# Expert products split by the parity of the input step, 512 columns wide, in a two-layer encoder trunk on one core

## The chip, the cores and the metric

The kernel runs on one core of one Trainium2 chip. The metric is the device time of one execution in microseconds (us); lower is better. Everything is computed in float32.

## What is computed

Two layers over 256 tokens of 1024 features: attention of three kinds with a projection in and out, then a mixture of 32 experts, of which each token uses two. The attention part matters here only as the work ahead of the experts; the experts are these lines of the reference:

```python
    g_p, g_sel = lax.top_k(g_prob, 1)
    ...
    e_p, e_sel = lax.top_k(jax.nn.softmax(e_logits, axis=-1), TOP_K_IN_GROUP)
    gate = g_p * e_p / jnp.sum(e_p, axis=-1, keepdims=True)
    ...
    def expert_block(args):
        xb, e = args
        h = jax.nn.silu(xb @ w_gate[e]) * (xb @ w_up[e])
        return h @ w_down[e]
    ...
    out = jax.ops.segment_sum(y, stok, num_segments=n)
```

`w_gate` and `w_up` are 1024 x 512 per expert, `w_down` is 512 x 1024. After the second layer the result is normalised and written out.

## The kernel before

Each layer has an attention stage and an expert stage. In the expert stage the 32 experts are taken in 4 rounds of 8 (`ROUNDS`, `BODY`), each round in two quads of 4 experts. Every expert has room for 32 tokens (`CAP`), so that the four experts of a quad fill 128 rows. There is a loop for experts with more than 32 tokens, which is entered only if there is one.

The order of the work is written out by hand, engine by engine, with semaphores between them. For an expert, TensorE (PE) does this, and in this order with the neighbours (lines 1909 to 1915): `products(e)`, `down_of(e - 1)`, `turned(e)`, `add(e - 1)`.

- `gate_up` (L1754 to L1771): for each of the 8 steps j of the input, four products with the same 32 tokens, each in its own group of 32 columns of the array and on its own 32 partitions of the bank `gu_ps`. The groups i = 0, 1 make the two halves of the gate's outputs, i = 2, 3 those of up, 256 columns each. So every group sums over all 8 steps.
- ScalarE (ACT) copies `gu_ps` to `h_rows`; `turns` (L1773) turns it by two transposes (L1777), and by two more products (L1779) the gate weights of this expert; ACT takes the exponential (L819), VectorE (DVE) makes silu times up in `hidden` (L1230 to L1233), then copies the turned gate weights to four groups of 32 partitions (L1236).
- `down` (L1783): for each of 4 chunks of the hidden vector, four groups of 32 columns, each with 256 of the 1024 outputs, into `tr`. ACT copies the result to `y` (128 x 256).
- `scatter` (L1794, products at L1799): for each of two tiles of 128 tokens, four products over 32 rows each, one for each 256 outputs, added to the sums that live in the four banks of `pj` and `lg` during the whole stage. A bank holds 256 outputs of both token tiles.

The sums are opened by `zero_sum` (L1701, products at L1703, which mark each bank as written) and `open_sum` on ACT (L774), which copies x in. The queue of SyncE (SP) issues the loads of the weights. An expert is 6144 KB. There are three places in the ring and one late place; experts 0 to 3 are loaded during attention. Expert 4's input half follows piece by piece as the first expert's steps are used (`REFILLS`, L503 to L507), and from then on a load waits for `gu_used` and `d_used` of the expert that held its place: ACT signals `d_used` when `down` of that expert has ended (L848). Two pieces of `w_down` of expert 2 lie where x lay and wait for `sums_open` and `rows_ready` (L498 to L501).

The last expert's `w_down` comes in four pieces of 512 KB with semaphores of their own (`last_in`, L577, L1787). After the last `scatter`, ACT and DVE read the sums: between the layers they copy them back to x (L889, L1330), which PE turns for the next layer (`turn_in`, L1464, L1470) once all is there, and at the end they square and weigh them in turns, half by half (L894, L1337). At two places per layer PE runs products of zeros, `keep_warm` (L1730).

Of the kernel before, what the change touches and what calls it, by code (L numbers as in the profile page):

```python
# [20 lines left out]
ALU = mybir.AluOpType  # L21
# [192 lines left out]
def trunk(nc, x_d, w_in_d, w_out_d, norm_mix, norm_ffn, bias_d, lam_q1, lam_k1, lam_q2, lam_k2,  # L214
# [3 lines left out]
    with ctx:  # L218
# [16 lines left out]
        h_ps = pv[:, 1, 0:2 * P].rearrange("p (c h s) -> p c h s", c=HALF // P, h=4)  # L235
# [31 lines left out]
        zeros = sb("zeros", P + 512, BF16)  # L267
# [51 lines left out]
        h_rows = take(HALF)  # L319
        y = take(D_MODEL // QUAD)  # L320
# [7 lines left out]
        hid = take(2 * P).rearrange("p (b c h s) -> p b c h s", b=2, c=HALF // P, h=2)  # L328
        e_neg = take(P).rearrange("p (c n) -> p c n", c=HALF // P)
        over_k = take(OVER)  # L330
        one0, cnt = over_k[:, 0:N_EXPERTS], over_k[:, N_EXPERTS:2 * N_EXPERTS]
        flags = lam_in.rearrange("p v d -> p (v d)")[:, 0:N_EXPERTS * MORE]
        codes = take(OVER)
        assert taken[0] <= 2048
        taken[0] = 2048
# [3 lines left out]
        chosen = take(TOK * N_EXPERTS).rearrange("p (t e) -> p t e", t=TOK)  # L339
        low = ARENA - 2 * SLOT - D_MODEL  # L340
# [20 lines left out]
        last_in = [sem(f"last_in{k}") for k in range(KE)]  # L361
# [102 lines left out]
        def _(sp):  # L464
# [3 lines left out]
            def first_experts(l):  # L468
# [46 lines left out]
            for l in range(DEPTH):  # L515
# [27 lines left out]
                for m in range(ROUNDS):  # L543
# [19 lines left out]
                    for kind, e in loads_of(m):  # L563
# [82 lines left out]
        def _(act):  # L646
# [20 lines left out]
            for l in range(DEPTH):  # L667
# [106 lines left out]
                def open_sum(t, half):  # L774

                    act.wait_ge(sums_zeroed, at(l, 4, 2 + 2 * half))
                    act.wait_ge(x_added, at(l, PARTS, (2, PARTS)[t] if half == 0 else 2 + t))
                    return copy(acc[t][half], x[:, t, 512 * half:512 * half + 512].rearrange("p (i c) -> p i c", i=2))
# [14 lines left out]
                for t in range(TOK):  # L793
# [4 lines left out]
                    else:  # L798
# [4 lines left out]
                        open_sum(0, 0)  # L803
# [14 lines left out]
                def neg_exp(b):  # L818
                    return nc.scalar.activation(e_neg, h_ps[:, :, 0:2, :].rearrange("p c h s -> p c (h s)"),  # L819
# [1196 lines left out]
```

## Time and profile before

| | us |
|---|---|
| median of 3 runs | 1163.73 |
| lowest and highest | 1161.87, 1165.86 |
| the profiled execution | 1163.3 |
| its span | 1161.4 |

| engine | busy us | share of the span |
|---|---|---|
| TensorE products (PE) | 923.6 | 80% |
| TensorE weight loads (PEld) | 581.4 | 50% |
| VectorE (DVE) | 417.7 | 36% |
| ScalarE (ACT) | 212.4 | 18% |

The profile was taken from one execution, which took 1163.3 us, 1.9 us more than its span. In the trace a float32 product appears as two matrix instructions, each with a weight load. A row of the timeline has the start and the length in us, the engine and the line, then the operation, what it writes and reads, its shape (rows x columns of the array, then partitions x columns of the moving operand) and the count; in brackets stands how long the engine was idle before it and what ended that.

### The profile page before, as it was taken

The numbers are of one execution on the slowest core, as the hardware profiler recorded it, in microseconds if no ns is written. First come the engines' busy times: TensorE is split into PE (matmuls) and PEld (weight loads), VectorE is DVE, ScalarE is ACT, GpSimd is POOL, SyncE is SP. The second block draws the span as 40 slices with busy tenths as digits, with TensorE's granted clock in tenths as the row PEclk, the third lists the DMA queues.
The fourth block names the chain that finished last, engine by engine and source line by source line (L and its number), as shares of the span: only waits on it lengthen the run. The fifth ranks groups of instructions, "written<-read, shape, count | busy, mean of one in ns | idle before, by whom it ended". The sixth has DMA issues, their size and how long they took to land.

```text
span 1161.4 us, 22055 instructions
## 1 busy us (share of the span) xinstructions
PE 923.6 (80%) x9540; PEld 581.4 (50%) x9547; DVE 417.7 (36%) x1180; ACT 212.4 (18%) x623; POOL 16.3 (1%) x38
## 2 busy tenths in 40 slices
PE   9999999776766576668899999997585857566786
PEld 5876666453434343435468766654343524334443
DVE  3656554421231222222337464554222222222223
ACT  2234332010101010101112442310110101001012
POOL 1000000000000000000010000000000000000000
PEclk9999999987888889879999999999888978898799
DMA  7966499999999999999996466999999999999996
GB/s 305 414 239 246 192 392 437 421 430 433 431 431 433 431 429 428 432 424 417 424 393 239 163 240 250 402 432 432 430 431 431 429 433 433 428 430 425 421 421 276
DMA packets 28116, 445.04 MB, mean 383 GB/s; under 512 B 8944, under 2 KB 10352, under 8 KB 14832
## 3 DMA queue, kind: packets, MB, share of 16 engines
q1 hardware_dynamic: 27456, 443.49, 90.6%
q8 instruction: 78, 1.28, 0.4%
q10 hardware_dynamic: 560, 0.10, 0.0%
q14 instruction: 22, 0.18, 0.0%
HBM read 442.53 MB, written 1.05 MB: 382 GB/s over the span
## 4 chain that ended last, share of the span: by engine, by line
DMA 50%; PE 45%; issue 1%; DVE 1%; ACT 1%; SPq 1%; POOL 0%; POOLq 0%; ACTq 0%; DVEq 0%
DMA ring_xb<-in_experts 44%; PE pv L1766 12%; PE pj L1391 8%; PE tr L1789 5%; DMA arena<-in_experts 3%; DMA ring_xb<-in_w_in_chunks 3%; PE pj L1397 2%; PE pj L1501 2%; PE pj L1621 2%; PE pj L1596 1%; PE pj L1799 1%; PE pj L1630 1%; PE lg L1421 1%; PE tr L1431 1%; PE pv L1779 1%
## 5 line engine op out<-in xcount | busy, mean ns | idle before, releaser
L1766 PE MATMUL pv<-ring_xb,xT 128*32 128x256 f32 x3840 | 286.8, 459 | 174.1 <-DMA ring_xb<-in_experts 173.9
L1766 PEld LDWEIGHTS pv<-ring_xb,xT 128*32 128x32 f32 x3840 | 136.2, 127 | 312.3 <-DMA ring_xb<-in_experts 189.9
L1230 DVE TENSOR_SCALAR arena<-arena 128x128 f32<-128x128 f32 x64 | 14.6, 228 | 562.7 <-ACT arena L819 562.7
L1789 PE MATMUL tr<-ring_xb,arena 128*32 128x256 f32 x1920 | 115.4, 379 | 17.8 <-issue 15.1
L649 ACT ACTIVATE arena<-pv 128x256 f32<-128x256 f32 x64 | 24.6, 385 | 491.2 <-PE pv L1766 491.2
L1236 DVE COPY arena<-pv 32x256 f32<-32x256 f32 x256 | 105.5, 412 | 2.6
L1391 PE MATMUL pj<-xT,ring_xb 128*128 128x256 f32 x448 | 100.1, 381 | 0.0
L1789 PEld LDWEIGHTS tr<-ring_xb,arena 128*32 128x32 f32 x1920 | 63.9, 109 | 61.2 <-issue 19.6
L1391 PEld LDWEIGHTS pj<-xT,ring_xb 128*128 128x128 f32 x448 | 84.1, 190 | 13.1 <-issue 1.1
L1799 PE MATMUL pj<-arena 32*128 32x256 f32 x512 | 72.5, 399 | 6.7 <-ACT arena L649 5.4
L1748 PE MATMUL tr<-arena,rows 128*128 128x128 f32 x448 | 60.6, 300 | 15.2 <-issue 10.5
L1799 PE MATMUL lg<-arena 32*128 32x256 f32 x512 | 72.5, 400 | 0.0
L649 ACT ACTIVATE arena<-tr 128x256 f32<-128x256 f32 (+3 forms) x106 | 41.3, 407 | 151.1 <-PE tr L1789 128.9
L1748 PEld LDWEIGHTS tr<-arena,rows 128*128 128x128 f32 x448 | 58.0, 213 | 20.1 <-issue 14.7
L1231 DVE RECIPROCAL arena<-arena 128x128 f32<-128x128 f32 x64 | 61.0, 953 | 2.2
L1799 PEld LDWEIGHTS pj<-arena 32*128 32x128 f32 x512 | 44.5, 184 | 23.2 <-issue 19.7
L649 ACT ACTIVATE xT<-tr,gains 128x128 f32<-128x128 f32 x128 | 36.6, 369 | 75.7 <-PE tr L1748 73.5
L1799 PEld LDWEIGHTS lg<-arena 32*128 32x128 f32 x512 | 43.7, 184 | 0.0
L1779 PE MATMUL pv<-con,arena 128*32 128x128 f32 x256 | 40.0, 279 | 0.0
L1777 PE MATMUL pv<-con,arena 128*128 128x128 f32 x128 | 32.4, 335 | 9.5 <-ACT arena L649 9.5
L1777 PEld LDWEIGHTS pv<-con,arena 128*128 128x128 f32 x128 | 20.3, 207 | 37.3 <-issue 19.8
L649 ACT ACTIVATE arena<-pj 64x256 f32<-64x256 f32 (+2 forms) x48 | 21.0, 442 | 72.7 <-PE pj L1391 52.2
(228 smaller groups left out, 807.5 us busy)
## 6 DMA issues: line engine op xcount, KB each, us to landing
ring_xb<-in_experts SPq DMA_DIRECT2D x48, 6144.0 KB, 22.1
ring_xb<-in_experts SPq DMA_DIRECT2D x18, 2048.0 KB, 13.3
ring_xb<-in_experts SPq DMA_DIRECT2D x6, 4096.0 KB, 28.0
ring_xb<-in_w_in_chunks SPq DMA_DIRECT2D x10, 2048.0 KB, 19.5
ring_xb<-in_w_out_halves SPq DMA_DIRECT2D x4, 2048.0 KB, 29.9
arena<-in_experts SPq DMA_DIRECT2D x2, 4096.0 KB, 12.8
ring_xb<-in_experts SPq DMA_DIRECT2D x8, 1024.0 KB, 9.6
arena<-in_experts SPq DMA_DIRECT2D x4, 2048.0 KB, 37.9
```

The source lines that it names most:

```text
L649: return nc.scalar.activation(out, in_, ACT.Copy, **k)
L1231: own.link(v.reciprocal(e_neg, e_neg))
L1236: ins = v.tensor_copy(pgT[k * CAP:(k + 1) * CAP, b].rearrange("p t s -> p (t s)"), pgt_ps[0:CAP])
L1391: ins = mm(out, w[:, j], xT[:, j, :], start=(j == 0), stop=(j == KD - 1))
L1397: ins = mm(out, src[:, j, t * P:(t + 1) * P], weights(i, n)[:, j, c:c + m], start=(j == 0), stop=(j == KD - 1))
L1501: ins = mm(bank[:, 0:R5], xT_raw[:, j, t * P:(t + 1) * P], weights(0, n5)[:, j, :], start=(j == 0), stop=(j == KD - 1))
L1748: ins = mm(wide_ps[:, j * n:(j + 1) * n], rows[:, t, j * P:(j + 1) * P], pick[:, t, 0:n], start=(t == 0), stop=(t == TOK - 1))
L1766: ins = mm(gu_ps[i * CAP:(i + 1) * CAP, :], xg[:, j, c:c + CAP], w, start=(j == 0), stop=(j == KD - 1), tile_position=(0, i * CAP), skip_g ...
L1777: turn_(h_ps[:, c].rearrange("p h s -> p (h s)"), by_step[:, c], ident)
L1779: ins = mm(pgt_ps[0:CAP, t * P:(t + 1) * P], pgate[:, t, i, :], ident, start=True, stop=True, tile_position=(0, 0), skip_group_check=True)
L1789: ins = mm(tr[i * CAP:(i + 1) * CAP, 0, 0:SEQ], hid[:, b, k % 2, k // 2, :], rows_of[k][:, SEQ * i:SEQ * (i + 1)], start=(k == 0), stop=(k ...
L1799: ins = mm(sums[i][:, SEQ * t:SEQ * (t + 1)], pgT[r, b, t, :], y[r, :], start=False, stop=last, tile_position=(i * CAP, 0), skip_group_che ...
```

## The change

- `gate_up`: each step makes two products of 512 columns, gate and up, in the column groups 0 and 2 on even steps and 1 and 3 on odd ones. Each group now sums over half the steps.
- `turns`: instead of two transposes, four products with `join`, a 128 x 64 matrix that turns a chunk of 128 and adds the two partial sums. The gate weights of a quad are turned once, at its first expert, for all four. `h_rows` and `y` are 512 wide.
- `down`: each chunk makes two products of 512 columns, again in groups by parity, and `scatter` multiplies over 64 rows, so that the two partial sums are added in it: one product per token tile and half.
- The sums: a bank holds one token tile and one half of the outputs. Three of the four `zero_sum` products go, since the banks are marked by earlier products, whose start flags are changed for that; a smaller one stays. `open_sum` for the upper halves is moved ahead of the second token tile's work on ACT, and `sums_open` is signalled once, after the lower halves.
- The last expert: the last piece of `w_down` is split in two, the lower half of the outputs is copied out and scattered ahead of the upper one, and what reads the sums waits for the bank it reads. At the end ACT and DVE take the banks in another order.
- `e_neg` goes (`hid` is used), `zeros` shrinks from 128 x 640 to 128 x 128 and is read repeatedly, and three products of zeros at the program's start go (L1487 to L1489).

```diff
-        sums = (pj[:, 0], pj[:, 1], lg[:, 0], lg[:, 1])
-        acc = tuple(tuple(bank[:, :, SEQ * t:SEQ * (t + 1)] for bank in (pj, lg)) for t in range(TOK))
+        acc = tuple(tuple(bank[:, t] for bank in (pj, lg)) for t in range(TOK))
-        gu_ps = pv[:, 0, 0:HALF]
+        gu_ps = pv[:, 0]
...
-        zeros = sb("zeros", P + 512, BF16)
+        zeros = sb("zeros", P, BF16)
...
-                    sp.wait_ge(sums_open, at(l, TOK, t + 1))
+                    sp.wait_ge(sums_open, l + 1)
...
-                            for k in range(KE):
+                            for k in range(KE - 1):
                                 sp.dma_start(spare[k], down_v[n][:, k]).then_inc(last_in[k], 16)
+                            for side in range(2):
+                                there = slice(512 * side, 512 * side + 512)
+                                sp.dma_start(spare[KE - 1][:, there], down_v[n][:, KE - 1, there]).then_inc(last_in[KE - 1 + side], 16)
...
                         open_sum(1, 0)
-                        open_sum(0, 0)
+                        open_sum(0, 0).then_inc(sums_open, 1)
...
-                    if t == 1:
-                        open_sum(0, 1).then_inc(sums_open, 1)
-                        open_sum(1, 1).then_inc(sums_open, 1)
-                    else:
+                    if t == 0:
+                        open_sum(0, 1)
+                        open_sum(1, 1)
                         gate_exps(0)
...
+                    def last_y_out(e):
+
+                        act.wait_ge(lower_down, l + 1)
+                        copy(y[0:64], tr[0:64, 0]).then_inc(lower_y, 1)
+                        act.wait_ge(wide_done, at(r, WIDE, y_use(e)))
+                        act.sem_inc(d_used[place(m * BODY + e)], 1)
+                        copy(y[64:128], tr[64:128, 1]).then_inc(wide_read, 1)
...
-            for t, half, weighted_first in ((0, 1, 0), (0, 0, 1), (1, 0, 1), (1, 1, 3)):
+            act.wait_ge(acc_done, at(DEPTH - 1, 2 * TOK, 1))
+            for t, half, weighted_first in ((0, 0, 0), (0, 1, 1), (1, 1, 1), (1, 0, 3)):
...
-                    for t, half, squared_first in ((0, 0, 0), (0, 1, 1), (1, 1, 1), (1, 0, 3)):
+                    dve.wait_ge(acc_done, at(l, 2 * TOK, TOK + 1))
+                    for t, half, squared_first in ((0, 1, 0), (0, 0, 1), (1, 0, 1), (1, 1, 3)):
...
-                if l == 0:
-                    for _ in range(3):
-                        mm(lg[:, 0], zeros[:, 0:P], zeros[:, P:P + 512], start=True, stop=True)
...
-                        for i in range(4):
-                            w = both[:, j, D_EXPERT * (i // 2):D_EXPERT * (i // 2 + 1)].rearrange("p (d c) -> p d c", c=KE)[:, :, KE // 2 * (i % 2):KE // 2 * (i % 2) + KE // 2]
-                            ins = mm(gu_ps[i * CAP:(i + 1) * CAP, :], xg[:, j, c:c + CAP], w,
-                                     start=(j == 0), stop=(j == KD - 1), tile_position=(0, i * CAP),
-                                     skip_group_check=True)
+                        for g in range(2):
+                            i = 2 * g + j % 2
+                            ins = mm(gu_ps[i * CAP:(i + 1) * CAP, :], xg[:, j, c:c + CAP],
+                                     both[:, j, D_EXPERT * g:D_EXPERT * (g + 1)], start=(j < 2), stop=(j >= KD - 2),
+                                     tile_position=(0, i * CAP), skip_group_check=True)
...
+                def turns(quad):
+
+                    by_chunk = h_rows.rearrange("q (p k) -> q k p", k=KE)
+                    for k in range(KE):
+                        ins = mm(h_ps[:, k].rearrange("p g s -> p (g s)"), by_chunk[:, k], join, start=True, stop=True,
+                                 skip_group_check=True)
+                    if quad:
+                        for t in range(TOK):
+                            ins = mm(pgt_ps[:, t * P:(t + 1) * P], pgate[:, t].rearrange("p e s -> p (e s)"), ident,
+                                     start=True, stop=True, skip_group_check=True)
+                    return ins
+
+                def down_part(rows_of, b, k, side, bank):
+
+                    i = 2 * side + k % 2
+                    return mm(tr[i * CAP:(i + 1) * CAP, bank], hid[:, b, k, :], rows_of[k][:, 512 * side:512 * side + 512],
+                              start=(k < 2), stop=(k >= KE - 2), tile_position=(0, i * CAP), skip_group_check=True)
...
+                def scatter_part(b, t, side, last):
+
+                    r = slice(64 * side, 64 * side + 64)
+                    return mm(acc[t][side], pgT[r, b, t, :], y[r, :], start=False, stop=last, tile_position=(64 * side, 0),
+                              skip_group_check=True)
```

Where the order moves: PE in the first expert stage, from `products(2)` on, with `down_of(1)`, `turned(2)` and `add(1)`. Before:

```order
L1766 MATMUL pv<-ring_xb,xT 32x256 [waits gu_full2]
L1766 MATMUL pv<-ring_xb,xT 32x256 x31
L1789 MATMUL tr<-ring_xb,arena 32x256 [waits wide_read,hid_ready,d_full1]
L1789 MATMUL tr<-ring_xb,arena 32x256 x15
L1777 MATMUL pv<-con,arena 128x128 [waits pgt_read,gu_read]
L1777 MATMUL pv<-con,arena 128x128
L1779 MATMUL pv<-con,arena 32x128 x2
L1799 MATMUL pj<-arena 128x256 [waits wide_read,pgt_read]
L1799 MATMUL pj<-arena 128x256
L1799 MATMUL lg<-arena 128x256 x2
L1799 MATMUL pj<-arena 128x256 x2
L1799 MATMUL lg<-arena 128x256 x2
```

The same place with the change (in it `gate_up` is L1785, `down` L1807, `turns` L1796 and `scatter` L1831):

```order
L1785 MATMUL pv<-ring_xb,xT 32x512 [waits gu_full2]
L1785 MATMUL pv<-ring_xb,xT 32x512 x15
L1807 MATMUL tr<-ring_xb,arena 32x512 [waits wide_read,hid_ready,d_full1]
L1807 MATMUL tr<-ring_xb,arena 32x512 x7
L1796 MATMUL pv<-arena 128x64 [waits pgt_read,gu_read]
L1796 MATMUL pv<-arena 128x64 x3
L1831 MATMUL pj<-arena 128x512 [waits wide_read,pgt_read]
L1831 MATMUL lg<-arena 128x512
L1831 MATMUL pj<-arena 128x512
L1831 MATMUL lg<-arena 128x512
```

The 60 products of an expert become 32, and the order of the four parts stays.

ACT ahead of the first expert, from the second tile's rows back to the first tile's (the copies `lg<-ring_xb` and `pj<-ring_xb` are `open_sum`). Before:

```order
L649 ACTIVATE rows<-ring_xb,rms 128x64x8
L788 ACTIVATE arena,lam_product<-arena,lam_product 128x4 [waits gmax_ready]
L791 ACTIVATE lam_product<-best 128x1 [waits emax_ready]
L649 ACTIVATE arena<-pj 128x512 [waits xnT_done]
L649 ACTIVATE xT<-tr 128x2x128 [waits xnT_done] x2
L649 ACTIVATE pj<-ring_xb 128x2x256 [waits x_added,sums_zeroed] x2
L649 ACTIVATE rows<-ring_xb,rms 128x64x8 [waits rms_ready,x_added]
L649 ACTIVATE rows<-ring_xb,rms 128x64x8
L649 ACTIVATE lg<-ring_xb 128x2x256 [waits x_added,sums_zeroed] x2
L649 ACTIVATE xT<-tr,gains 128x128 [waits wide_done]
```

With the change:

```order
L652 ACTIVATE rows<-ring_xb,rms 128x64x8
L652 ACTIVATE lg<-ring_xb 128x512 [waits x_added,mix_read,lg_read] x2
L796 ACTIVATE arena,lam_product<-arena,lam_product 128x4 [waits gmax_ready]
L799 ACTIVATE lam_product<-best 128x1 [waits emax_ready]
L652 ACTIVATE arena<-pj 128x512 [waits xnT_done]
L652 ACTIVATE xT<-tr 128x2x128 [waits xnT_done] x2
L652 ACTIVATE pj<-ring_xb 128x512 [waits x_added,xnT_read,sums_zeroed] x2
L652 ACTIVATE rows<-ring_xb,rms 128x64x8 [waits rms_ready,x_added]
L652 ACTIVATE rows<-ring_xb,rms 128x64x8
L652 ACTIVATE xT<-tr,gains 128x128 [waits wide_done]
```

The two copies to `lg` have moved ahead of the gate's exponentials, and nothing stands any more between the last `rows` copy and the first gathered tokens.

PE at the last expert of a layer, from its `down` on, with the change (before, the four pieces had four products of 256 columns each, and the eight products of `scatter` followed, all behind one wait for `y`):

```order
L1807 MATMUL tr<-xT,arena 32x512 [waits last_in0,wide_read,hid_ready]
L1807 MATMUL tr<-xT,arena 32x512
L1807 MATMUL tr<-arena 32x512 [waits last_in1]
L1807 MATMUL tr<-arena 32x512
L1807 MATMUL tr<-lowrank,arena 32x512 [waits last_in2]
L1807 MATMUL tr<-lowrank,arena 32x512
L1807 MATMUL tr<-arena 32x512 [waits last_in3]
L1807 MATMUL tr<-arena 32x512 [waits last_in4]
L1831 MATMUL pj<-arena 128x512 [waits lower_y,pgt_read]
L1831 MATMUL pj<-arena 128x512
L1831 MATMUL lg<-arena 128x512 [waits wide_read]
L1831 MATMUL lg<-arena 128x512
```

The last two rows of `scatter` wait for the upper half alone.

## Rows read from the trace of the kernel before

**Rows 1.** The profile's page: GB/s by slice, the queue that loads instructions

```profile
GB/s 305 414 239 246 192 392 437 421 430 433 431 431 433 431 429 428 432 424 417 424 393 239 163 240 250 402 432 432 430 431 431 429 433 433 428 430 425 421 421 276
...
q8 instruction: 78, 1.28, 0.4%
```

**Rows 2.** The chain of waits in order of time: start, length, what

```profile
202.78 19.51 DMA ring_xb<-in_experts
...
543.63 38.29 DMA ring_xb<-in_w_in_chunks
```

**Rows 3.** Windows: stretch, its us, busy of PE, PEld, DVE, ACT, POOL, clock, DMA share, GB/s

```profile
155.00:160.00 5.00, 4.90 (x63) 3.36 (x66) 2.70 (x15) 3.69 (x13) 0.00 (x0) 1.00 0.81 238
730.00:735.00 5.00, 4.90 (x63) 3.33 (x66) 2.79 (x16) 3.52 (x13) 0.00 (x0) 1.00 0.94 338
230.00:520.00 290.00, 194.94 (x2426) 116.11 (x2430) 73.20 (x187) 31.32 (x97) 0.00 (x0) 0.83 1.00 429
```

**Rows 4.** Timeline, PE on experts 3 to 5, and a gather in the last round

```profile
193.17 0.61 PE L1789 MATMUL tr<-xT,arena 128*32 128x256 f32 x8
...
195.00 0.51 PE L1777 MATMUL pv<-con,arena 128*128 128x128 f32 x2
...
195.99 0.48 PE L1799 MATMUL pj<-arena 32*128 32x256 f32 x2
...
197.07 3.83 PE L1766 MATMUL pv<-ring_xb,xT 128*32 128x256 f32 x64
...
200.72 1.91 PE L1789 MATMUL tr<-ring_xb,arena 128*32 128x256 f32 x32
...
1101.00 3.84 PE L1748 MATMUL tr<-arena,rows 128*128 128x128 f32 x32
```

**Rows 5.** Timeline at the second expert: tiles of two kinds of products side by side

```profile
162.77 0.43 PE L1766 MATMUL pv<-ring_xb,xT 128*32 128x256 f32 x3
...
162.87 0.27 PE L1779 MATMUL pv<-con,arena 128*32 128x128 f32 x1
```

**Rows 6.** Timeline, the load of expert 7 and PE at expert 6, both layers

```profile
207.82 1.51 PE L1766 MATMUL pv<-ring_xb,xT 128*32 128x256 f32 x16 [3.13 <-DMA ring_xb<-in_experts]
777.60 0.33 SPq L570 DMA_DIRECT2D ring_xb<-in_experts  x1
781.98 1.51 PE L1766 MATMUL pv<-ring_xb,xT 128*32 128x256 f32 x12 [2.47 <-DMA ring_xb<-in_experts]
```

**Rows 7.** Loads and stores by line: times, KB each, median us from issue to landing

```profile
out<-rows SPq DMA_DIRECT2D x2, 512.0 KB, 3.1
```

**Rows 8.** Timeline, SP's loads ahead of the first experts

```profile
155.54 2.37 SPq L501 DMA_DIRECT2D ring_xb<-in_experts  x2
...
157.96 2.12 SPq L505 DMA_DIRECT2D ring_xb<-in_experts  x3
```

**Rows 9.** Timeline, the program's start

```profile
5.50 1.49 PE L1489 MATMUL lg<-zeros 128*128 128x512 bf16 x3
...
15.73 0.61 PE L1484 MATMUL lg<-arena,con 128*128 128x128 f32 x4
```

**Rows 10.** Timeline, ACT copying 512 columns out of `tr`

```profile
136.23 0.60 ACT L649 ACTIVATE arena<-tr 128x512 f32<-128x512 f32 x1
```

**Rows 11.** Timeline, from the last expert of layer 0 to layer 1

```profile
574.82 0.64 PE L1789 MATMUL tr<-xT,arena 128*32 128x256 f32 x8
...
581.96 6.17 PE L1501 MATMUL pj<-ring_xb,rows 128*128 128x440 f32 x16 [0.39 <-DMA ring_xb<-in_w_in_chunks]
```

**Rows 12.** Timeline, the end of layer 1

```profile
1149.14 0.64 PE L1789 MATMUL tr<-xT,arena 128*32 128x256 f32 x8
...
1150.49 0.64 PE L1789 MATMUL tr<-arena 128*32 128x256 f32 x8
1151.28 0.39 ACT L649 ACTIVATE arena<-tr 128x256 f32<-128x256 f32 x1 [3.37 <-PE tr L1789]
...
1155.12 0.60 ACT L894 ACTIVATE arena<-lg 128x512 f32<-128x512 f32 x1
```

More of the change, by code:

```diff
@@ L1212, in weigh @@
                     own.mark(v.tensor_copy(cnt, pv[:, 1, 64:96]))
+                    groups = ident.rearrange("p (g j s) -> p g j s", g=2, j=2)
+                    own.mark(v.tensor_tensor(join.rearrange("p (g s) -> p g s", g=2), groups[:, :, 0, :], groups[:, :, 1, :], ALU.add))
                     rank(1)
@@ L1462, in _ @@
                 for _ in range(8 if l == 0 else 4):
[L1463 removed]
+                    mm(tr[:, 0].rearrange("p (n c) -> p n c", n=KE), zeros, spread(zeros, 1, KE), start=True, stop=True)
                 def turn_in(t):
@@ L1699, in gather_first @@
                     return ins
-                def zero_sum(i):
-                    mm(sums[i], zeros[:, 0:P], zeros[:, P:P + 512], start=True, stop=False,
-                       skip_group_check=True).then_inc(sums_zeroed, 1)
                 out_upper(1, 1)
@@ L1732, in keep_warm @@
                     for _ in range(n):
-                        mm(sums[0], zeros[:, 0:P], zeros[:, P:P + 512], start=False, stop=False,
+                        mm(pj[:, 0].rearrange("p (n c) -> p n c", n=KE), zeros, spread(zeros, 1, KE), start=False, stop=False,
                            skip_group_check=True)
@@ L1771, in gate_up @@
                     return ins
-                def turns(i):
-                    by_step = h_rows.rearrange("q (p c) -> q c p", c=HALF // P)
-                    for c in range(HALF // P):
-                        turn_(h_ps[:, c].rearrange("p h s -> p (h s)"), by_step[:, c], ident)
-                    for t in range(TOK):
-                        ins = mm(pgt_ps[0:CAP, t * P:(t + 1) * P], pgate[:, t, i, :], ident, start=True, stop=True,
-                                 tile_position=(0, 0), skip_group_check=True)
-                    return ins
@@ L1794, in scatter @@
-                def scatter(b, last=False):
-                    for t in range(TOK):
-                        for i in range(4):
-                            r = slice(i * CAP, (i + 1) * CAP)
-                            ins = mm(sums[i][:, SEQ * t:SEQ * (t + 1)], pgT[r, b, t, :], y[r, :],
-                                     start=False, stop=last, tile_position=(i * CAP, 0), skip_group_check=True)
-                            if last and t == TOK - 1:
-                                ins.then_inc(acc_done, 1)
+                def turns(quad):
[8 more added lines that the diff above has]
+                    return ins
@@ new lines, in down @@
+                def down(rows_of, b):
+                    for k in range(KE):
+                        for side in range(2):
+                            ins = down_part(rows_of, b, k, side, 0)
+                    return ins
+                def scatter_part(b, t, side, last):
+                    r = slice(64 * side, 64 * side + 64)
+                    return mm(acc[t][side], pgT[r, b, t, :], y[r, :], start=False, stop=last, tile_position=(64 * side, 0),
+                              skip_group_check=True)
@@ L1803, in scatter @@
+                def scatter(b):
+                    for t in range(TOK):
+                        for side in range(2):
+                            ins = scatter_part(b, t, side, False)
                     return ins
@@ L1875, in add, with down_and_add_last @@
                         if m == 0 and e == 0:
-                            pe.wait_ge(sums_open, at(l, TOK, TOK))
-                        scatter(e % 2, m == ROUNDS - 1 and e == BODY - 1)
+                            pe.wait_ge(sums_open, l + 1)
+                        scatter(e % 2)
+                    def down_and_add_last(e):
+                        pe.wait_ge(hid_ready, at(r, BODY, e + 1))
+                        pe.wait_ge(wide_read, at(r, READS, y_read(e) - 1))
+                        down_last(e % 2)
+                        pe.wait_ge(pgt_read, at(r, BODY, e + 1))
+                        pe.wait_ge(lower_y, l + 1)
+                        for side in range(2):
+                            if side == 1:
+                                pe.wait_ge(wide_read, at(r, READS, y_read(e)))
+                            for t in range(TOK):
+                                scatter_part(e % 2, t, side, True).then_inc(acc_done, 1)
                     if m == ROUNDS - 1:
```

130 lines of the change are left out of this document (71 added, 59 removed).

## The prediction

> **What bounds the kernel now.** I read the page first. Its GB/s by slice are near 430 in most slices and fall to 163 to 250 in two stretches, the attention stages [rows 1]; from 230 to 520 us the transfers run at 429 GB/s with their engines busy all the time, while PE is busy 195 of 290 us [rows 3]. The chain of waits says the same from the end: in the expert stages its long pieces are loads of `experts`, and one of 38.3 us (the weights of the next layer) leads into layer 1 [rows 2]. So an expert costs what its 6144 KB take, 6.29 MB / 429 GB/s = 14.7 us, and what PE saves in that stretch is waiting time. PE sets the time in five places only: the program's start and the attention stages; the first steps of the first expert, which free the ring; the first six experts, four of them already loaded, which PE takes at its own pace while each frees the place of a later one; the way from the last expert into layer 1; and the end.
>
> **The change, part by part,** against the profiled execution (1163.3 us, span 1161.4; the median of the runs is 0.4 above it).
>
> *PE per expert.* Matrix instructions in four column groups run four at a time: in `down` 32 of 256 columns take 1.91 and 8 take 0.61, so 24 more take 1.30, or 0.43 for eight, and 0.18 is the tail [rows 4]. `gate_up` has 64 in 3.83 [rows 4]. With the change it has 32 of twice the length, and four neighbours still lie in four groups (0, 2, 1, 3): 32 x 0.108 + 0.18 = 3.65, which saves 0.18. `down` keeps its array time, 1.9. The four parts of `turns` took 195.99 - 195.00 = 0.99; eight instructions with full weights at the gather's 3.84 / 32 = 0.12 make 0.96, and at the first expert of a quad four more, 0.48 [rows 4]. `scatter` took 197.07 - 195.99 = 1.08 [rows 4] with 16 instructions in four row groups, 0.86 of it array time at the rate above. Over 64 rows only two groups exist: two rows of four instructions, 0.43 each, make 1.72. That is 0.86 more. Sum: -0.18 - 0.03 + 0.86 = +0.65 us per expert, so PE becomes slower, not faster. In the loading stretch, with some 4 us or more idle per expert, this costs nothing.
>
> That two 64-row products overlap at all is seen on no row; the nearest are the column groups above. The Trainium skill (TensorEngine Tiling (Array Packing), Tiling Modes) gives two tiles for 64 rows and four for 32, so by it too this product loses half of its overlap.
>
> *The burst of the first six experts.* The load of expert 7 waits for `down` of expert 4. Until then PE has done six `gate_up` (-1.1), five `turns` (-0.15 and twice +0.48) and four `scatter` (+3.4): +3.1. The load was issued at 202.78 in layer 0 [rows 2] and at 777.60 in layer 1, and the load ahead of it had landed when PE began expert 6, at 207.82 and 781.98 [rows 6]. The 512 KB output takes 3.1 us to land, of which 1.2 is transfer, so a load needs some 1.9 ahead [rows 7]. It must be issued by 205.9 and 780.1; with +3.1 it comes at 205.9 and 780.7. I take +0.5 for both layers; bounds 0 and, with PE 1.5 slower per expert in place of 0.65, +4 per layer.
>
> *Earlier loads ahead of the burst.* SP issued the two pieces over x at 155.54, behind the sums' opening, and the first refills at 157.96 [rows 8]. From 155 to 160 only 238 GB/s flowed, which is 5 x (429 - 238) / 429 = 2.2 us lost, and 1.1 in 730 to 735 [rows 3]. With the lower sums opened first, the pieces can go after 152.5 and 154.6. But the refills behind them still wait for the first steps of `gate_up`, whose 512-column products end some 0.4 later. The gap moves more than it closes: -0.3 per layer, bounds 0 and the whole 3.3. The products of zeros and the copies that go or move here lie beside the router's chain on DVE and PE.
>
> *The start.* Three products of zeros (1.49) go, but at 15.73 PE needs a product of x's norm, which DVE and ACT make from a load of x and not from PE's work [rows 9]. I take it that this norm comes some 0.3 ahead of PE: -0.3, bounds 0 and -1.5.
>
> *Into layer 1.* `y` of 512 columns takes ACT 0.60 in place of 0.39 [rows 10, 12]. So `scatter` of the last but one expert starts 0.2 later and takes 0.86 longer: `down` of the last starts at 574.82 + 1.1 = 575.9 [rows 11]. Its four chunks go in two pairs of 0.86: results at 577.8. ACT copies both halves by 579.1, `scatter` of the upper half ends about 580.3 and 581.1, the copies back at 581.0 and 581.8, and PE turns the second tile (8 x 0.12 and a tail) from about 582.0: layer 1 starts at 583.1, not at 581.96 when its weights landed [rows 11]. +1.1; bounds -0.4 (the idle time there) and +2.
>
> *The end.* Before, `down` of the last expert started at 1149.14, its last piece came at 1150.49, and the last sum was squared from 1155.12 [rows 12]. Now, as in layer 0, `down` from 1150.15, results at 1152.0, two copies to 1153.4, the lower `scatter` from 1152.9 and the upper beside it from 1153.5 to 1155.4. The first square starts at 1154.0, but three more in turns with DVE follow the upper half, the last from 1156.8: +1.7. The last piece's arrival no longer decides, so splitting it buys nothing. Bounds: -0.5 (half a piece) and +3.
>
> The upper `scatter` can start beside the lower only if tiles overtake. They do: three instructions of `gate_up` start at 162.77, ahead of an L1779 at 162.87 that precedes them in the program [rows 5]. The Trainium skill (TensorE: Matmul & The Clock Gate, The mechanism) says that matmuls start and end strictly in program order. By that the upper one would wait for the lower one's last start, and this term would be +2.3; the row differs, and I go by it.
>
> *Instructions loaded.* They are 1.28 MB in all [rows 1]; about a fifth go: -0.3 us, bounds 0 and -1.
>
> **Sum:** +0.5 - 0.6 - 0.3 + 1.1 + 1.7 - 0.3 = **+2.1**, that is 1165.4 for the profiled execution and **1165.8** for the median. A measurement of this kernel tells about 0.3%, 3.5 us, from no change.
>
> **The rivals.**
>
> *Faster: the ring is what counts.* If the early pieces close the gaps (-3.3), PE is not late for expert 7 (0), the start gives -1.3, and both ends are set by arrivals as now (+0.3 together), the sum with the instructions' -0.3 is about -4.6: 1159.1. For it: the 238 GB/s, and the idle 0.39 for DMA ahead of layer 1 [rows 11]. Against it: the refills behind the pieces, and 1.1 us more work on PE ahead of the last `down`. 0.18.
>
> *Slower: expert 7's load.* Between `down`, `turns`, `scatter` and `gate_up` the array changes its division four times per expert. If that, or a slower 64-row product, makes an expert 1.5 us longer than before, `down` of expert 4 is over 7 us later, and transfers stand still for about 4.5 in each layer: 1165.8 + 8 = 1174. It decides from about 3 us of lateness on, and the forecast is at 3.1. Before, the changes cost little: 0.2 between `scatter` and `gate_up`. The Trainium skill (TensorEngine Tiling (Array Packing), Key Properties) says that a change of tiling mode drains the engine; it gives no price. 0.18.
>
> *Slower: the groups do not overlap at 512 columns.* Then `gate_up` takes about 6.9 and `down` 3.4, an expert costs 12.7 of PE's time, the burst is some 26 us longer, less 3 of slack: 23 per layer, near 1213. Nothing speaks for it except that neighbours now have different weights. 0.04.
>
> **How the numbers follow.** The forecast has 0.60; rivals 0.18, 0.18, 0.04. Of the forecast, 0.02 lies under -3.5 and 0.06 over +3.5: faster 0.20, same 0.52, slower 0.28. The range takes in most of the first two rivals and the bounds of the terms near the ends: 1159.5 to 1172.
>
> **What would show it.** Right: `gate_up` at 3.6 to 3.7 warm, `down` 1.9, `scatter` 1.7 to 1.9; PE's busy time little changed though its instructions fall by nearly half; the GB/s in the long stretch still 429; the load of expert 7 three us later after the first `gate_up` than before; PE, not a load, ahead of layer 1; and 12 to 13 us between the landing of the last piece and the end (now 11). Wrong: a gap in GB/s behind expert 6, or PE waiting for the last piece again.

## The result, and the profile after

The changed kernel takes **1181.9 us** (median of 4 runs, 1181.67 to 1183.22) against 1163.18 beside it: a ratio of 1.0157, 95% interval 1.0144 to 1.0170, or 18.7 us. The forecast was 1165.8 with a range up to 1172. Further down, the numbers in brackets behind a time are its ratio to the kernel before, measured beside it, and the 95% interval of that ratio.

| | before | after |
|---|---|---|
| span of the profiled execution | 1161.4 | 1180.0 |
| PE busy | 923.6 | 1031.4 |
| instructions, all engines | 22055 | 15268 |
| ACT busy | 212.4 | 240.9 |

PE executes far fewer instructions and is busy 108 us longer. The page of the changed kernel, with its GB/s to be held against [rows 1]:

```profile
PE 1031.4 (87%) x6146; PEld 552.2 (47%) x6146; DVE 423.9 (36%) x1182; ACT 240.9 (20%) x625; POOL 15.8 (1%) x38
...
GB/s 307 402 234 264 206 390 404 347 436 436 428 432 433 436 429 425 436 425 424 421 393 199 167 204 289 398 336 421 424 435 429 435 429 434 434 431 428 430 423 218
```

The eighth slice fell from 421 to 347 (and the seventh from 437 to 404), and one of layer 1 from 432 to 336. The windows of the changed kernel, with the columns of [rows 3], show the two places, the long stretch, and the pieces ahead of the burst:

```profile
200.00:204.00 4.00, 4.00 (x26) 2.82 (x20) 0.00 (x0) 1.09 (x3) 0.00 (x0) 1.00 0.97 418
204.00:208.00 4.00, 4.00 (x32) 1.19 (x32) 3.71 (x9) 0.08 (x1) 0.00 (x0) 1.00 0.19 78
208.00:212.00 4.00, 4.00 (x33) 1.75 (x25) 2.10 (x8) 1.19 (x2) 0.00 (x0) 1.00 0.00 0
...
200.00:220.00 20.00, 20.00 (x144) 8.75 (x136) 10.95 (x30) 3.23 (x7) 0.00 (x0) 1.00 0.65 264
780.00:800.00 20.00, 20.00 (x148) 8.94 (x144) 8.68 (x23) 3.66 (x9) 0.00 (x0) 1.00 0.64 255
...
230.00:520.00 290.00, 232.60 (x1436) 107.64 (x1424) 75.94 (x189) 40.28 (x99) 0.00 (x0) 0.88 1.00 431
...
155.00:160.00 5.00, 4.90 (x40) 2.78 (x44) 2.93 (x17) 2.65 (x11) 0.00 (x0) 1.00 0.88 322
```

Read the last column. Before, both 20 us stretches ran at 427 GB/s:

```profile
200.00:220.00 20.00, 15.56 (x220) 8.91 (x212) 10.86 (x31) 2.10 (x6) 0.00 (x0) 0.91 1.01 427
780.00:800.00 20.00, 14.57 (x214) 8.29 (x214) 8.94 (x27) 1.43 (x4) 0.00 (x0) 0.91 1.00 427
```

So 20 x (427 - 264) / 427 = 7.6 us of transfer are lost in layer 0 and 8.1 in layer 1, at expert 7's load. PE is busy throughout both. The long stretch stands at 431 GB/s as before, though PE works 233 of its 290 us and not 195 [rows 3]. The timeline says why the burst is late. One expert of it, to be held against [rows 4], and the issue of expert 7's load in each layer:

```profile
164.49 3.64 PE L1785 MATMUL pv<-ring_xb,xT 128*32 128x512 f32 x32
167.95 1.90 PE L1807 MATMUL tr<-ring_xb,arena 128*32 128x512 f32 x16
169.78 2.08 PE L1796 MATMUL pv<-arena 128*128 128x64 f32 x8
171.79 0.69 PE L1831 MATMUL pj<-arena 64*128 64x512 f32 x1
...
173.18 0.59 PE L1831 MATMUL pj<-arena 64*128 64x512 f32 x1
...
211.12 0.33 SPq L570 DMA_DIRECT2D ring_xb<-in_experts  x1
...
794.71 0.33 SPq L570 DMA_DIRECT2D ring_xb<-in_experts  x1
```

L1785 is `gate_up`, L1807 `down`, L1796 the join in `turns`, L1831 `scatter`. The join holds PE for 171.79 - 169.78 = 2.01 us, where the forecast had 0.96. `scatter` takes 1.91, `gate_up` 3.46 from start to start. The next expert begins at 173.70, 9.21 us behind 164.49; over the whole burst it is 9.21 to 9.22. Before, an expert took 7.56, from this row to 197.07 [rows 4]:

```profile
189.51 3.83 PE L1766 MATMUL pv<-ring_xb,xT 128*32 128x256 f32 x64
```

By expert 4's `down` that makes the load 8.3 us late (211.12, not 202.78 [rows 2]).

The rest is at the end. In windows of 2 us the expert transfers die out between 1148 and 1152 before (the first two rows) and between 1162 and 1166 after (the other two), 14 us later; the span grew by 18.6:

```profile
1148.00:1150.00 2.00, 1.94 (x32) 1.32 (x36) 0.02 (x1) 0.00 (x0) 0.00 (x0) 1.00 0.56 221
1150.00:1152.00 2.00, 1.32 (x24) 0.51 (x20) 0.00 (x0) 0.39 (x1) 0.00 (x0) 1.00 0.14 57
...
1162.00:1164.00 2.00, 2.00 (x18) 0.42 (x16) 1.87 (x5) 0.00 (x0) 0.00 (x0) 1.00 0.64 246
1164.00:1166.00 2.00, 1.11 (x8) 0.55 (x6) 1.43 (x4) 0.60 (x1) 0.00 (x0) 1.00 0.22 88
```

So about 4.6 lie behind the last transfer:

```profile
1145.36 1.92 PE L1807 MATMUL tr<-ring_xb,arena 128*32 128x512 f32 x16 [0.64 <-DMA ring_xb<-in_experts]
1147.22 2.08 PE L1796 MATMUL pv<-arena 128*128 128x64 f32 x8
...
1151.15 2.33 PE L1753 MATMUL pj<-zeros 128*128 128x512 bf16 x10
1153.41 1.92 PE L1785 MATMUL pv<-arena,xT 128*32 128x512 f32 x16
1155.27 1.47 PE L1753 MATMUL pj<-zeros 128*128 128x512 bf16 x6
1156.66 1.92 PE L1785 MATMUL pv<-arena,xT 128*32 128x512 f32 x16
1159.39 2.08 PE L1796 MATMUL pv<-arena 128*128 128x64 f32 x8 [0.80 <-ACT arena L652]
```

From 1145.36 on no row of PE waits for a transfer. The products of `keep_warm` (L1753), which filled waits before, now stand in PE's way, and the join is there twice. `keep_warm` has three places at the end of a layer, not two: ten, six and four products.

### The profile page after: what moved, and what is told of

Same layout as the page of the kernel before. It is cut to its first block, busy times and chain, and to the rows that moved or that the text cites. A ratio compares the mean times of both kernels' runs of the same rounds, so it can differ in the third digit from the quotient of the medians.

```text
span 1180.0 us, 15268 instructions
## 1 busy us (share of the span) xinstructions
PE 1031.4 (87%) x6146; PEld 552.2 (47%) x6146; DVE 423.9 (36%) x1182; ACT 240.9 (20%) x625; POOL 15.8 (1%) x38
## 4 chain that ended last, share of the span: by engine, by line
PE 56%; DMA 40%; issue 1%; ACT 1%; DVE 1%; SPq 0%; POOL 0%; POOLq 0%; ACTq 0%; DVEq 0%
DMA ring_xb<-in_experts 39%; PE pv L1785 14%; PE pj L1420 8%; PE tr L1807 7%; PE pv L1796 4%; PE pj L1831 4%; PE pj L1426 2%; PE tr L1767 2%; PE pj L1647 2%; PE pj L1527 1%; PE pj L1622 1%; PE pj L1656 1%; PE lg L1450 1%; DMA ring_xb<-in_x 1%; ACT arena L652 1%
## 5 line engine op out<-in xcount | busy, mean ns | idle before, releaser
L1785 PE MATMUL pv<-ring_xb,xT 128*32 128x512 f32 x1920 | 269.8, 711 | 102.9 <-DMA ring_xb<-in_experts 102.7
L1785 PEld LDWEIGHTS pv<-ring_xb,xT 128*32 128x32 f32 x1920 | 65.1, 127 | 283.4 <-issue 147.3
L1796 PEld LDWEIGHTS pv<-arena 128*128 128x128 f32 x512 | 124.3, 327 | 67.6 <-ACT arena L652 65.9
L1796 PE MATMUL pv<-arena 128*128 128x64 f32 x512 | 133.2, 403 | 12.8 <-ACT arena L652 12.8
L1831 PE MATMUL pj<-arena 64*128 64x512 f32 x256 | 130.8, 632 | 9.0 <-ACT arena L652 9.0
L1831 PE MATMUL lg<-arena 64*128 64x512 f32 x256 | 131.1, 633 | 0.0
L1807 PE MATMUL tr<-ring_xb,arena 128*32 128x512 f32 x960 | 114.5, 595 | 5.7 <-issue 3.8
L652 ACT ACTIVATE arena<-tr 128x512 f32<-128x512 f32 (+4 forms) x108 | 56.1, 537 | 144.1 <-PE tr L1807 121.8
L1831 PEld LDWEIGHTS pj<-arena 64*128 64x128 f32 x256 | 44.1, 191 | 52.8 <-issue 48.4
L1807 PEld LDWEIGHTS tr<-ring_xb,arena 128*32 128x32 f32 x960 | 29.6, 110 | 83.6 <-issue 79.8
L1831 PEld LDWEIGHTS lg<-arena 64*128 64x128 f32 x256 | 44.1, 191 | 0.5 <-issue 0.5
```

The costliest lines, as they stand in the source:

```text
L652: return nc.scalar.activation(out, in_, ACT.Copy, **k)
L1785: ins = mm(gu_ps[i * CAP:(i + 1) * CAP, :], xg[:, j, c:c + CAP], both[:, j, D_EXPERT * g:D_EXPERT * (g + 1)], start=(j < 2), stop=(j >= KD ...
L1796: ins = mm(h_ps[:, k].rearrange("p g s -> p (g s)"), by_chunk[:, k], join, start=True, stop=True, skip_group_check=True)
L1807: return mm(tr[i * CAP:(i + 1) * CAP, bank], hid[:, b, k, :], rows_of[k][:, 512 * side:512 * side + 512], start=(k < 2), stop=(k >= KE - 2 ...
L1831: return mm(acc[t][side], pgT[r, b, t, :], y[r, :], start=False, stop=last, tile_position=(64 * side, 0), skip_group_check=True)
```

## The experiments

**Theory A:** the join is dear because its weights lie 16 bytes apart; this and `scatter` slow the burst, expert 7's load comes late, and transfers stand still. **Rivals:** B, the join is dear because its products are short or full-sized between narrow tiles; C, PE's longer work costs by itself, and the gap is only its shadow.

### The join's weights

The first edit lets ACT lay `h_rows` down chunk by chunk:

```diff
-                        copy(h_rows, gu_ps).then_inc(gu_read, 1)
+                        copy(h_rows.rearrange("q (k p) -> q p k", k=KE), gu_ps.rearrange("q (p k) -> q p k", k=KE)).then_inc(gu_read, 1)
...
-                    by_chunk = h_rows.rearrange("q (p k) -> q k p", k=KE)
+                    by_chunk = h_rows.rearrange("q (k p) -> q k p", k=KE)
```

> The changed kernel, but ACT writes h_rows chunk by chunk, so that the join's weights lie side by side instead of 16 bytes apart. Theory A (the stride of the weights makes the join dear, 0.26 us an instruction, and the long burst releases expert 7's load late): the eight join instructions fall from 2.08 us to 0.95 to 1.05, an expert of the burst from 9.22 to 8.15, expert 7's load is issued at 205.8 instead of 211.1, about 2.4 us of transfer are lost in each layer instead of 7.7 to 8.0, and with 1 us at each layer's way out the time is 1167 to 1170. Rival B (the join is dear because its products are short or because full and narrow tiles alternate, not because of the stride): join still 2.0 us or more, time 1181 to 1183.

Measured: 1169.78 us (1.0056, 1.0040 to 1.0073). The join takes 1.03 to the next start, an expert 8.24, the load is issued at 206.63. **12.1 us of the 18.7 come back by one access pattern.** Rival B is out. PE's weight loads for the join show it by themselves, in the changed kernel and in this run: 327 ns each against 191.

```profile
L1796 PEld LDWEIGHTS pv<-arena 128*128 128x128 f32 x512 | 124.3, 327 | 67.6 <-ACT arena L652 65.9
...
L1796 PEld LDWEIGHTS pv<-arena 128*128 128x128 f32 x512 | 61.9, 191 | 75.0 <-ACT arena L652 73.3
```

Lost transfers were more than expected: both stretches ran at 352 GB/s, 3.5 us each.

The same by itself, on the array alone, behind the last `scatter`:

```diff
                         down_and_add_last(BODY - 1)
+                        if l == DEPTH - 1:
+                            by4 = h_rows.rearrange("q (p k) -> q k p", k=4)
+                            by2 = h_rows.rearrange("q (p k) -> q k p", k=2)
+                            by1 = h_rows.rearrange("q (k p) -> q k p", k=4)
+                            for _ in range(4):
+                                mm(pv[:, 0, 0:64], by1[:, 0], join, start=True, stop=True)
...
```

> The changed kernel with nine groups of four products behind its last scatter, on the same h_rows, whose result nobody reads: weights side by side, 8 bytes apart, 16 bytes apart, each with 64 columns of join, with 128 columns of ident, and as transposes. Theory A: an instruction with weights side by side takes 0.11 to 0.14 us whatever the columns, with 16 bytes apart 0.25 to 0.26, with 8 bytes apart between the two or like 16. Rival B: 64 columns cost no less than 0.25 with weights side by side too. Time about 10 us over the changed kernel's.

The probe's timeline; the lines stand in the order by1, by2, by4, for 64 columns, for 128, and as transposes:

```profile
1171.39 1.10 PE L1987 MATMUL pv<-arena 128*128 128x64 f32 x8
1172.34 1.11 PE L1989 MATMUL pv<-arena 128*128 128x64 f32 x8
1173.28 2.03 PE L1991 MATMUL pv<-arena 128*128 128x64 f32 x8
1175.14 1.11 PE L1993 MATMUL pv<-con,arena 128*128 128x128 f32 x8
1176.09 1.11 PE L1995 MATMUL pv<-con,arena 128*128 128x128 f32 x8
1177.03 2.03 PE L1997 MATMUL pv<-con,arena 128*128 128x128 f32 x8
1178.90 0.60 PE L1999 MATMUL pv<-con,arena 128*128 128x128 f32 x4
1179.33 0.64 PE L2001 MATMUL pv<-con,arena 128*128 128x128 f32 x4
1179.81 0.64 PE L2003 MATMUL pv<-con,arena 128*128 128x128 f32 x4
```

From start to start, eight instructions take 0.95 us with weights side by side, 0.94 with weights 8 bytes apart and 1.86 with 16 bytes: 0.12, 0.12 and 0.23 us each, the same for 64 and 128 columns. That 8 bytes cost nothing was not expected. Four transposes take 0.43 and 0.48 to the next start with the turned data side by side and 8 bytes apart, and the row for 16 bytes is as long as the one for 8 (0.64). So the old `turns` (L1777 in [rows 4]), transposes that read 8 bytes apart, could not have shown it. The probe's 1182.52 us, 0.6 over the changed kernel and not 10, is no price: its products lie beside the kernel's tail on other engines.

The Trainium skill (Advanced Engine Details and Errata, Memory Cachelines) says that SBUF is read in lines of 16 bytes and that at least two accesses must fall into a line to hide its latency. The trace agrees for weights: two float32 in a line are free, one in a line costs twice.

In that first mending ACT wrote with a jump of 512 bytes between elements, and its copy took 1.08 us. The other walk, `q k p` on both sides, reads PSUM 16 bytes apart and writes in a row:

> As join_contiguous, but ACT walks h_rows in the order it is written and PSUM 16 bytes apart; in join_contiguous it wrote 16-byte neighbours 512 bytes apart and took 1.08 us where the copy took 0.60. In best_try the copy of this form took 0.60. Theory A: join 0.95 and copy 0.60, an expert of the burst as in join_contiguous (the copy lies beside PE's work) 8.2 us, and 0.5 us less for each last expert whose copy PE waits for: 1168.5 to 1169.8. Rival: the copy's 0.48 us is never waited for: 1169.8 as before.

Measured: 1167.89 (1.0040, 1.0025 to 1.0055), 1.9 us less, more than Theory A had. ACT's rows, of the first mending and of `best_try`, which walks the same way as this run:

```profile
L652 ACT ACTIVATE arena<-pv 128x512 f32<-128x512 f32 x64 | 69.1, 1080 | 472.8 <-PE pv L1785 472.8
```

```profile
L652 ACT ACTIVATE arena<-pv 128x512 f32<-128x512 f32 x64 | 38.2, 597 | 465.9 <-PE pv L1785 465.9
```

Reading PSUM with a stride costs ACT nothing here (597 ns, as in the changed kernel); writing SBUF with one costs 0.48 us. The same section of the Trainium skill also warns of strided PSUM access, but for matmuls, which no run here shows.

### The late load

> The changed kernel, but expert 7's load is two: its gate and up as soon as expert 4's gate_up has been read, its down behind expert 4's down. PE's work is untouched, 9.22 us an expert. Theory A (the loss is the standstill of the transfers ahead of expert 7): no window between 200 and 230 nor between 780 and 810 below 400 GB/s, 7.7 + 8.0 us back, 1165 to 1168. Rival C (the loss is PE's own longer work over the whole stage, and the standstill only its shadow): the gap closes, but the time stays above 1176.

```diff
-        return order + [("all", e) for e in range(AHEAD + 2, last)]
+        return order + [("all", AHEAD + 2), ("gu", BODY - 1), ("d", BODY - 1)]
...
-D_LOADS = {1: 1, 2: 3, AHEAD: 1, AHEAD + 1: 1, LAST - 2: 1, LAST - 1: 1}
+D_LOADS = {1: 1, 2: 3, AHEAD: 1, AHEAD + 1: 1, BODY - 1: 1, LAST - 2: 1, LAST - 1: 1}
```

Measured: 1174.68 (1.0096, 1.0079 to 1.0113): 7.2 back and not 14 to 17, a miss. Both stretches recovered only to 405 and 394 GB/s; 215 to 225 ran at 359 and 795 to 805 at 360, ahead of expert 8's load, which waits for expert 5's `down` in the same way (issued at 220.11). The next load was late next. Rival C's 1176 or more did not come either.

> load7_split with expert 8's load split as well (its gate and up behind expert 5's gate_up, ahead of expert 7's down). load7_split stood at 1174.7 where 1165 to 1168 was expected, and its transfers fell to 387 and 331 GB/s in 215 to 225 and again by 795 to 805, ahead of expert 8's load, issued at 220.1. Theory A: these gaps go, 2 to 2.5 us in each layer: 1169 to 1171. Rival D (what load7_split kept is not there but at the ways out, the join and 4.8 us of keep_warm on a PE that no longer waits): 1173 to 1175.

Expert 8's load was split in the same way. Measured: 1171.96 (1.0079, 1.0064 to 1.0094), another 2.7. The transfers are nearly whole, PE is busy all the time, and yet 8.5 us over the kernel before remain:

```profile
200.00:220.00 20.00, 20.00 (x148) 8.90 (x143) 10.71 (x30) 2.94 (x6) 0.00 (x0) 1.00 1.00 428
780.00:800.00 20.00, 20.00 (x139) 9.63 (x138) 10.94 (x30) 2.95 (x6) 0.00 (x0) 1.00 0.99 425
```

The time lies between what Theory A (up to 1171) and Rival D (from 1173) had, so neither number came. The gap is worth about 10 of the 18.7, and the remainder lies where D has it: layer 1 begins at 584.76 and not 581.96, and the last transfers end some 2 us later than before but the span 8.1 later.

> Both edits together. Theory A: standstill gone by the split, and the join's 1.05 us back wherever PE is not covered: the way into layer 1, the start of layer 1's burst and the end, some 1 us each: 1162 to 1165, near the kernel before (1163.2). Rival C: above 1172. Rival B: as load7_split, 1165 to 1168.

Measured: 1164.99 (1.0010, 1.0000 to 1.0019), at the upper end of Theory A. The two mendings overlap: 12.1 and 7.2 alone, 16.9 together, since both shorten the same standstill.

Lateness without any of the new products, in the kernel before:

```diff
-                        turn_(h_ps[:, c].rearrange("p h s -> p (h s)"), by_step[:, c], ident)
+                        for _ in range(9):
+                            turn_(h_ps[:, c].rearrange("p h s -> p (h s)"), by_step[:, c], ident)
```

> The kernel before, with each of an expert's two transposes issued nine times over instead of once: 16 more instructions, at the 0.11 us that the probe's transposes took, 1.7 to 1.8 us more of PE for each expert and no other difference. Theory A (it is the lateness of the burst that costs, whatever makes it late): an expert of the burst 9.3 us, expert 7's load 8 to 9 us later than 202.8, 6 to 8 us without transfers in each layer, and about as much again at the ways out: 1178 to 1184. Rival C (the new products or joined banks cost by themselves): 1163 to 1168, since the old products are all still there and PE has 95 us free in the 290 of the long stretch.

> The same slowed kernel before, with expert 7's load split as in load7_split. Theory A: the standstill at expert 7 goes and a shorter one is left before expert 8, as in load7_split: 6 to 8 us less than before_slowed, 1171 to 1176. Rival C: no difference between the two.

Measured: **1187.86** (1.0211, 1.0196 to 1.0226) and **1178.14** (1.0134, 1.0119 to 1.0148). An expert takes 9.5 to 9.7 us, more than the 9.3 expected; both times lie some 2 to 4 us over what was written, and the difference is 9.7, not 6 to 8. Expert 7's load is issued at 212.07, 9.3 late. Windows of the first of the two:

```profile
200.00:204.00 4.00, 4.00 (x57) 2.80 (x50) 0.00 (x0) 0.77 (x2) 0.00 (x0) 1.00 1.05 455
204.00:208.00 4.00, 4.00 (x59) 2.60 (x61) 2.22 (x6) 0.28 (x1) 0.00 (x0) 1.00 0.28 115
208.00:212.00 4.00, 4.00 (x73) 2.11 (x66) 3.60 (x11) 0.39 (x1) 0.00 (x0) 1.00 0.02 4
...
200.00:220.00 20.00, 20.00 (x292) 13.11 (x288) 10.33 (x28) 2.29 (x7) 0.00 (x0) 1.00 0.67 267
```

The old products, slowed, give the same hole, and splitting one load gives back 9.7 of the 24.4 us without touching PE. Rival C, in the form written for these two runs (the new products cost by themselves, and the split changes nothing), is out. What the split leaves is in part the same loss again: 215 to 225 still runs at 334 GB/s, 795 to 805 at 357. In the unsplit run the last transfers die out between 1168 and 1174, some 20 us later than before, and the span grew by 24.7. **PE's 16 extra instructions cost mostly through the transfers that they delay.**

### What the rest belongs to

`half_change` puts only `gate_up` by parity, the join (weights side by side) and `pgate` once a quad into the kernel before:

> The kernel before with the gate_up and join part of the change alone (512-column gate_up by parity, join of partial sums with weights side by side, pgate once a quad), and its own down, y, scatter, sums, start and end. It tells what of the 6.4 us that join_contiguous still lacks to the kernel before belongs to scatter and the ends. Theory A (scatter's 0.83 us an expert and PE's way out): an expert of the burst 7.4 to 7.6 us, expert 7's load at 202 to 203.5, no standstill, 1162 to 1165. Rival E (it belongs to gate_up by parity or the join): 1167 or more.

Measured: 1162.90 (0.9994, 0.9985 to 1.0003). An expert takes 7.41 us, expert 7's load goes out at 202.87, the stretch runs at 419. So none of the loss is in those parts. What `join_psum_read` still lacks, 4 to 5 us, lies in what this run leaves out: `scatter` over 64 rows and what belongs to it (`down` by parity, the longer `y`, the sums, the end). These weren't taken apart.

> The changed kernel with chunk-major h_rows, read from PSUM 16 bytes apart by ACT or written so, whichever the copy makes of it, both loads split, and two of the three keep_warm runs at each layer's last experts cut to one product (4.2 + 0.8 us of PE less in each layer, of which both_mended could use about 1, since its second piece of the last gate and up lands at about 1140.5). both_mended was 1165.0. Theory A: 1 us in each layer from keep_warm and up to 1 from the loads: 1162 to 1164, within 0.3% of the kernel before. If the clock falls at the waits that keep_warm filled, up to 3 us more: 1165 to 1168.

> best_try with keep_warm as in the changed kernel. best_try was 1163.3 with runs from 1162.1 to 1169.3, and its clock stood at 0.80 to 0.85 in the last stretches of both layers. Theory A (PE is the limit there, and its clock with it): steadier, 1163 to 1164.5. If the shorter keep_warm was worth its microsecond all the same: 1164 to 1165.

> best_warm with the first keep_warm run of the last experts cut from ten products to five (1.1 us less of PE) and the others as they were. Theory A: 1162 to 1163.5 if the clock holds, 1163 to 1165 if it falls as in best_try. Either way within 0.3% of the kernel before, which would say that this design has no time to win while the transfers of the long stretch set the pace.

All three have the PSUM walk and both loads split. Measured: 1163.31 (1.0005, 0.9994 to 1.0016) with runs from 1162.13 to 1169.27, 1162.61 (0.9995, 0.9986 to 1.0004), and 1163.08 (0.9996, 0.9987 to 1.0005). With two of the three runs of `keep_warm` cut to one product each (`best_try`) the time spreads over 7 us and its profiled execution, one of the longest (1168.89), had the granted clock at 0.83 and 0.85 in 560 to 580 and 1140 to 1150, where it stood at 1.00 before. With all of them, or with five products of the ten, it spreads over 3.5 and 2.5 us. That the clock makes the spread is not shown: over a whole execution the mean granted clock was 0.927 in the shortest run (1162.13) and in the longest (1169.27). None beats the kernel before by what can be told. In `best_warm` the last transfers end some 3 us earlier than before, and PE's longer way out gives it all back.

## Why the prediction was wrong

**The step that failed** is a term of *PE per expert*: "eight instructions with full weights at the gather's 3.84 / 32 = 0.12 make 0.96". They take 2.01. The gather's weights lie side by side, the join's 16 bytes apart, and the price was carried over without looking at the access pattern. The sum of +0.65 an expert was 9.22 - 7.56 = +1.66. With the join mended it is 8.24 - 7.56 = +0.68, so the other terms of that part held: `gate_up` -0.18 (measured -0.19, 3.46 against 3.65 from start to start), `down` 0, `scatter` +0.86 (+0.83).

**A second term failed** and stood hidden behind the first: the load of expert 7 "must be issued by 205.9", 3.1 us of slack, from PE's start on expert 6 less 1.9. `before_slowed` shows where the transfers die out, and that they flow again about a microsecond after the load's issue at 212.07:

```profile
204.00:205.00 1.00, 1.00 (x10) 0.88 (x9) 0.00 (x0) 0.00 (x0) 0.00 (x0) 1.00 1.00 410
205.00:206.00 1.00, 1.00 (x15) 0.77 (x17) 0.30 (x2) 0.28 (x1) 0.00 (x0) 1.00 0.12 49
...
213.00:214.00 1.00, 1.00 (x11) 1.00 (x9) 0.00 (x0) 0.00 (x0) 0.00 (x0) 1.00 2.69 786
```

So the last byte ahead of the gap came about 205.1, and the load had to go by 204.1: 1.3 of slack. For the kernel before, that is an estimate, good to some half a microsecond: up to 205 both runs moved 318 GB/s on the mean. PE's start on expert 6, at 207.82, came 2.7 us behind that last byte, and an issue needs 1.0 to the first byte: 3.7 together, where the forecast took 1.9 from the store of 512 KB [rows 7]. With the PE terms as forecast (`join_psum_read`) the load was still 3.4 us late, and the two stretches ran at 347 and 367 GB/s: 3.7 and 2.8 us lost, not 0.5 together. The gap behind expert 6 is what the prediction itself had named as a sign of being wrong.

The terms beside each other, against the span of before. The fourth and fifth rows are what is left over: of layer 1's start (590.54 and 583.80, not 581.96), and of the whole.

| term | forecast | changed kernel | `join_psum_read` |
|---|---|---|---|
| start | -0.3 | -0.3 | -0.3 |
| earlier pieces, both layers | -0.6 | -1.0 | -1.0 |
| expert 7's load, both layers | +0.5 | +15.7 | +6.5 |
| into layer 1 | +1.1 | +2.2 | -0.5 |
| layer 1's other parts and the end | +1.7 | +2.0 | -0.1 |
| instructions loaded | -0.3 | in the two rows above | in the two rows above |
| sum | +2.1 | +18.6 | +4.6 |

So of the 16.1 us that the forecast missed by, 14.0 are the join (1181.90 - 1167.89) and 2.1 the rest, in which 6.0 too little for the load stand against three terms forecast too dear. That the mended kernel comes within 2.1 us of the forecast is therefore in part luck.

**The rival "Slower: expert 7's load"** (1174, chance 0.18) named the mechanism, the place and an expert 1.5 us longer, and blamed changes of the array's division or a slow 64-row product; neither was it, since `scatter` cost what was forecast. It was undersized: 7.6 and 8.1 us and not 4.5 in each layer. The rival "groups don't overlap" is refuted by `gate_up` at 3.64 (its 12.7 for an expert is also too low by its own terms, 6.9 + 3.4 + 0.96 + 1.72 = 13.0). The rival "Faster" needed all 3.3 us of the early gaps and a PE in time for expert 7, and had neither. And PE's busy time was not "little changed": it grew by 108 us, and by 43 with the join mended (966.3), which is what +0.65 for each of 64 experts gives.

**Earlier pieces** did come in layer 0: 322 GB/s for 238 in 155 to 160, 1.0 us. In layer 1 nothing is seen of it: counted from each layer's own start, 130 to 182 us into it, 2.3 us of transfer were lost before, 2.7 in the changed kernel and 2.2 in `join_psum_read`. And the queue then runs dry sooner at expert 7, about 203.6 in `join_psum_read`, which is part of what the load's row lost.

**Into layer 1 and the end** cost more in the changed kernel and less with the join mended than forecast. Between the two lies the join alone, 2.7 and 2.1 us; it stands twice on each way out. How much `keep_warm` takes, 4.6 us of products that I left among the waits they used to fill, is open, since with less of it nothing was won that can be told. The overtaking that the end's term rests on did come. The upper `scatter` (into `lg`) starts ahead of products into `pj` that precede it in the program:

```profile
1169.71 1.09 PE L1831 MATMUL pj<-arena 64*128 64x512 f32 x2 [0.79 <-ACT arena L652]
1170.23 0.69 PE L1831 MATMUL lg<-arena 64*128 64x512 f32 x1
1170.64 0.59 PE L1831 MATMUL pj<-arena 64*128 64x512 f32 x1
```

**The long stretch** was right: 431 GB/s, and 38 us more of PE in it cost nothing.

## What to carry to other kernels

Price a product by the nearest row with the same access pattern of its weights, not only the same shape: here, in float32, one element in 16 bytes doubled it. Where an engine frees the buffers of a stream that the transfers bound, the first byte of the next load must come before the last byte of the one ahead; the moment at which a consumer starts is too late a mark (here by 2.7 us). And when the consumer becomes the limit, look at filler work in its stream: it is surely free only in waits.

## What the runs showed of the hardware

- A float32 product with 128 x 128 weights, an instruction: 0.12 us with weights side by side or 8 bytes apart, 0.23 with 16 bytes, for 64 or 128 moving columns (`join_probe`). The mean weight load of the join was 327 ns at 16 bytes and 191 side by side. Transposes take 0.11 to 0.12 side by side and 8 bytes apart, and the row at 16 bytes is as long as the one at 8.
- ACT's copy of 128 x 512 from PSUM: 0.60 us, the same when PSUM is read 16 bytes apart, 1.08 when SBUF is written 512 bytes apart.
- Two 64-row products do overlap: L1831 into `pj` and `lg` at 171.79 both, and the next pair 0.43 to 0.53 later. Products in different groups of rows also overtake each other: one into `lg` starts at 1170.23, ahead of one into `pj` at 1170.64 that precedes it in the program.
- `keep_warm` at one product for ten and one for four spread the time over 7 us, where the same kernel with all of it spreads over 3.5, with a lower granted clock in two stretches of the profiled execution (0.83 and 0.85); the cause of the spread is not shown.
